# The MLP of a two-layer diffusion trunk in plain fp32: one product for three, hidden groups of 512 for 256

## The chip, the cores and the metric

The kernel runs on one core of one Trainium2 chip. The metric is the device time of one execution in microseconds. A core has a matrix engine (TensorE, PE in the rows, with PEld for its weight loads), a vector engine (DVE), a scalar engine (ACT), GpSimd (POOL) and SyncE (SP), which here issues nearly all the DMAs. Each engine runs its own program in order; they wait for one another through semaphores.

## What is computed

Two layers (DEPTH = 2) over 1152 tokens: 1024 latent ones and a prompt of 128, at D_MODEL = 1024 and a hidden width of 4096. A layer mixes the tokens (attention, mLSTM, neighbourhood attention, one output projection) and then runs the part that matters here:

```python
def squared_relu_mlp(h, w_up, w_down):
    return jnp.square(jax.nn.relu(h @ w_up)) @ w_down

def trunk_layer(x, mods, mixer, g_pre_mix, g_post_mix, g_pre_ffn, g_post_ffn, w_up, w_down):
    sh1, sc1, gt1, sh2, sc2, gt2 = mods
    mix_out, extras = mixer(rms_norm(x, g_pre_mix) * (1 + sc1) + sh1)
    x = x + gt1 * rms_norm(mix_out, g_post_mix)
    h = rms_norm(x, g_pre_ffn) * (1 + sc2) + sh2
    x = x + gt2 * rms_norm(squared_relu_mlp(h, w_up, w_down), g_post_ffn)
    return x, extras
```

All inputs, weights and outputs are fp32.

## The kernel before

The tokens lie in NT = 9 tiles of P = 128 (the prompt is the last), and D in KD = 8 slices of 128. The layers are one loop of two turns; within a layer, stages follow each other, each a block in which every engine has its own piece of program, with all engines meeting between blocks. The stages that the change touches come last in a layer:

- `out_projection` (L1612): turns the mixer's output, splits it into a high part (rounded to the type F32R) and a low part (what is left), and multiplies with W_out, split in the same way. At its end SP also loads the first 256 columns of W_up into `raw_up` (L1629); ACT and POOL split them (L1699, L1634), so that they lie ready for the MLP.
- `residual_norm("mix", 0, True)` (L457): a software pipeline over the nine tiles. For a tile, DVE scales the mixer's output (L557), adds the residual (L560), normalises (L567); PE turns the tile (L602); ACT and DVE modulate four of its eight slices each (L521, L575) into `full`, a buffer of three tiles. Then ACT copies the tile's high part into `hi` (L528) and DVE subtracts it to get `lo` (L582). Each step of a tile stands one turn of the loop behind the one ahead of it (ADD 1, SQUARES 2, NORM 3, MODULATE 4, HIGH 5, LOW 6).
- `mlp` (L1702): the hidden width goes in NG = 16 groups of HID = 256. In a group, six up tiles are made, each 128 hidden columns by 384 tokens, over KD = 8 slices; ACT takes relu (L1785) and square (L1787) and splits off the high part (L1789), DVE the low part (L1807). Then 18 down tiles, 128 tokens by 512 output columns, over KH = 2 slices, which DVE adds to `mix` (L1813). Each product of two fp32 operands is made by three F32R matmuls: high by high, high by low, low by high (L1755, L1769). The weights of a group have one buffer: SP loads them raw (L1723, L1726), ACT copies out the high parts (L1779, L1796) and POOL subtracts for the low parts (L1734, L1740); the next load waits for that. PE, ACT, DVE and POOL run the groups as loops; SP's issues are written out.
- `residual_norm("mlp", 1, False)`: the last residual add.

The three matmuls of an up product are:

```python
for k in range(KD):
    for a, b in ((up_hi, hi), (up_hi, lo), (up_lo, hi)):
        mm = pe.matmul(ps[:, j % 3, 0:384], a[:, k, m * P:(m + 1) * P], b[:, k, n * 384:(n + 1) * 384], ...)
```

Elsewhere the kernel multiplies plain fp32 operands by a single call, for example in the neighbourhood mixer's input projection (L1020, 128 columns of weights by 384 tokens over eight slices, six tiles a block, three blocks a layer), its v projection (L1027, 128 by 128) and the mLSTM's (L1167, as L1020).

Of the kernel before, what the change touches and what calls it, by code (L numbers as in the profile page):

```python
# [48 lines left out]
HID = 256  # L49
# [73 lines left out]
def build(nc, I, O):  # L123
    sems = {}
    with ExitStack() as ctx:
# [91 lines left out]
        with nc.Fori(0, DEPTH) as l:  # L217
# [239 lines left out]
            def residual_norm(tag, sub, norm):  # L457
# [4 lines left out]
                with ExitStack() as own:  # L462
# [4 lines left out]
                    FULL = 3  # L467
                    full = sb(f"{tag}_h_full", [P, FULL, KD, P], own) if norm else None
# [3 lines left out]
                    if norm:  # L472
                        x_sq, x_rstd = sem(f"{tag}_x_squares"), sem(f"{tag}_x_rstd")
                        normed, turned = sem(f"{tag}_normed"), sem(f"{tag}_turned")
                        mod_d, mod_a = sem(f"{tag}_modulated_dve"), sem(f"{tag}_modulated_act")
                        hi_done, lo_done = sem(f"{tag}_hi_done"), sem(f"{tag}_lo_done")
                    ON_DVE = 4

                    ADD, SQUARES, NORM, MODULATE, HIGH, LOW = 1, 2, 3, 4, 5, 6
                    STEPS = NT + (LOW if norm else ADD)  # L480
# [6 lines left out]
                    with nc.Block() as block:  # L487
# [17 lines left out]
                        def _(act):  # L505
# [9 lines left out]
                            def modulate(t):  # L515
                                c = 1 if t == PROMPT else 0
                                act.wait_ge(turned, t + 1)
                                if t >= FULL:
                                    act.wait_ge(lo_done, t - FULL + 1)
# [5 lines left out]
                            def high_part(t):  # L525
                                act.wait_ge(mod_a, t + 1)
                                act.wait_ge(mod_d, t + 1)
                                act.copy(hi[:, :, t * P:(t + 1) * P], full[:, t % FULL, :, :]).then_inc(hi_done, 1)  # L528

                            for n in range(STEPS):  # L530
                                if n < NT:
                                    squares_y(n)
                                if norm and 0 <= n - HIGH < NT:
                                    high_part(n - HIGH)
# [19 lines left out]
                        def _(dve):  # L554
# [14 lines left out]
                            def modulate(t):  # L569
                                c = 1 if t == PROMPT else 0  # L570
                                dve.wait_ge(turned, t + 1)
                                if t >= FULL:
                                    dve.wait_ge(lo_done, t - FULL + 1)
# [5 lines left out]
                            def low_part(t):  # L579
                                dve.wait_ge(hi_done, t + 1)  # L580
                                tt = slice(t * P, (t + 1) * P)
                                dve.tensor_tensor(lo[:, :, tt], full[:, t % FULL, :, :], hi[:, :, tt].bitcast(F32), ALU.subtract).then_inc(lo_done, 1)  # L582

                            for n in range(ADD, STEPS):
                                if n - ADD < NT:
                                    add_residual(n - ADD)
                                if norm and 0 <= n - LOW < NT:
                                    low_part(n - LOW)
# [1023 lines left out]
            def out_projection():  # L1612
# [5 lines left out]
                with ExitStack() as own:  # L1618
                    raw = sb("w_out_raw", [P, 2, KD, CUT], own)
                    w_hi = sb("w_out_hi", [P, 2, KD, CUT], own, F32R)  # L1620
                    w_lo = sb("w_out_lo", [P, 2, KD, CUT], own, F32R)
                    with nc.Block() as block:
                        @block.sync
                        def _(sp):
# [4 lines left out]
                            sp.dma_start(raw_up[:, :, :], w_up[:, :, 0:HID]).then_inc(sem("m_up_loaded"), 16)  # L1629

                        @block.gpsimd
                        def _(pool):
                            pool.wait_ge(sem("m_up_hi"), 1)
                            pool.tensor_tensor(up_lo[:, :, :], raw_up[:, :, :], up_hi[:, :, :].bitcast(F32), ALU.subtract).then_inc(sem("m_up_lo"), 1)  # L1634
# [41 lines left out]
                        def _(act):  # L1676
# [14 lines left out]
                            for j in range(NCUT * NT):  # L1691
# [5 lines left out]
                                if t == NT - 1 and c == NCUT - 2:  # L1697
                                    act.wait_ge(sem("m_up_loaded"), 16)
                                    act.copy(up_hi[:, :, :], raw_up[:, :, :]).then_inc(sem("m_up_hi"), 1)  # L1699


            def mlp():  # L1702
# [8 lines left out]
                with ExitStack() as own:  # L1711
                    raw_down = sb("w_down_raw", [P, KH, D], own)
                    down_hi, down_lo = (sb(f"w_down_{x}", [P, KH, D], own, F32R) for x in ("hi", "lo"))
                    u_hi, u_lo = (sb(f"u_{x}", [P, KH, TOK], own, F32R) for x in ("hi", "lo"))
                    relu = sb("relu", [P, 2, 384], own)
                    square = sb("square", [P, 2, 384], own)
                    with nc.Block() as block:
                        @block.sync
                        def _(sp):
                            for g in range(NG):  # L1720
                                if g >= 1:
                                    sp.wait_ge(sem("m_up_lo"), g)
                                    sp.dma_start(raw_up[:, :, :], w_up[:, :, g * HID:(g + 1) * HID]).then_inc(sem("m_up_loaded"), 16)  # L1723
                                if g >= 1:
                                    sp.wait_ge(sem("m_down_lo"), g)
                                sp.dma_start(raw_down[:, :, :], w_down[g]).then_inc(sem("m_down_loaded"), 16)  # L1726

                        @block.gpsimd
                        def _(pool):
                            pool.memset(mix[:, :, :], 0.0).then_inc(sem("m_out_cleared"), 1)  # L1730

                            def down_low(g):
                                pool.wait_ge(sem("m_down_hi"), g + 1)
                                pool.tensor_tensor(down_lo[:, :, :], raw_down[:, :, :], down_hi[:, :, :].bitcast(F32), ALU.subtract).then_inc(sem("m_down_lo"), 1)  # L1734

                            with pool.Fori(0, NG - 1) as g:
                                down_low(g)

# [162 lines left out]
```

## Time and profile before

| | before |
|---|---|
| time, median of 2 runs (lowest, highest) | 4337.26 us (4336.97, 4337.55) |
| span of the profiled execution | 4341.4 us |
| PE busy in it | 3953.9 us (91%) |
| DVE busy | 1637.1 us (38%) |
| ACT busy | 1242.6 us (29%) |
| POOL busy | 781.1 us (18%) |
| the costliest line, L1755 (up products), three groups | 515.0 + 514.6 + 514.4 us busy |
| L1769 (down products), three groups | 448.8 + 448.7 + 448.1 us busy |

The profiled execution's span is 4.1 us longer than the median. PE's busy times add up to more than the time that its matmuls fill, since successive matmuls overlap in the records: what a matmul costs in a stream is the interval from one start to the next, not its recorded duration. The rows give tenths of busy time in 40 slices, and the clock that the TensorE was granted (PEclk, as a share of 2.4 GHz; the other level is half of that).

### The profile page before, as it was taken

How to read it: one execution, taken by the hardware profiler on the slowest of the kernel's cores; microseconds unless marked ns; L12 is line 12 of the kernel's file. 1: busy time of each engine (PE TensorE's matmuls, PEld its weight loads, DVE VectorE, ACT ScalarE, POOL GpSimd, SP SyncE). 2: the span in 40 equal slices, each digit the busy share in tenths (PEclk: the TensorE clock that was granted, in tenths of full speed). 3: DMA queues.
4: the chain of work that ended last, by engine and by line, in shares of the span. 5: the costliest groups of instructions: out<-in, count | busy, mean ns of one | idle time of the engine just before them, and what ended most of it. 6: DMA issues, size and time to landing. Idle time of an engine off the chain costs nothing. (4 is left out here: it accounts for less than half of the span.)

```text
span 4341.4 us, 54476 instructions
## 1 busy us (share of the span) xinstructions
PE 3953.9 (91%) x21270; PEld 3248.0 (75%) x21270; DVE 1637.1 (38%) x3077; ACT 1242.6 (29%) x2544; POOL 781.1 (18%) x565
## 2 busy tenths in 40 slices
PE   6799999999697999999777999999896879999997
PEld 4477777674696999999644777777746869999996
DVE  1644333323716333333416443332237153333334
ACT  2233222212425222222222332222124242222222
POOL 0300111201304112121203001112013141211212
PEclk9899999999997999999887999899999979999998
DMA  6100111004113111111241001110041131111112
GB/s 204 52 1 1 44 44 28 25 19 156 31 41 111 42 39 48 39 39 48 84 158 52 1 1 44 44 32 29 13 155 31 50 105 39 39 48 39 48 39 87
DMA packets 189240, 233.44 MB, mean 54 GB/s; under 512 B 41522, under 2 KB 167092, under 8 KB 187444
## 3 DMA queue, kind: packets, MB, share of 16 engines
q1 hardware_dynamic: 188916, 231.04, 16.9%
q8 instruction: 112, 1.84, 0.2%
q14 instruction: 68, 0.56, 0.0%
q10 hardware_dynamic: 144, 0.01, 0.0%
HBM read 210.84 MB, written 32.71 MB: 56 GB/s over the span
## 5 line engine op out<-in xcount | busy, mean ns | idle before, releaser
L1813 DVE TENSOR_TENSOR mix<-mix,ps 128x512 f32<-128x512 f32 x576 | 395.3, 688 | 344.1 <-PE ps L1769 344.1
L1755 PE MATMUL ps<-h_hi,w_up_hi 128*128 128x384 f32 x1536 | 515.0, 335 | 10.0 <-PEq L487 10.0
L1755 PE MATMUL ps<-h_hi,w_up_lo 128*128 128x384 f32 x1536 | 514.6, 335 | 0.0
L1755 PE MATMUL ps<-h_lo,w_up_hi 128*128 128x384 f32 x1536 | 514.4, 335 | 0.0
L1769 PE MATMUL ps<-w_down_hi,u_lo 128*128 128x512 f32 x1152 | 448.8, 390 | 0.0
L1769 PE MATMUL ps<-w_down_lo,u_hi 128*128 128x512 f32 x1152 | 448.7, 390 | 0.0
L1769 PE MATMUL ps<-w_down_hi,u_hi 128*128 128x512 f32 x1152 | 448.1, 389 | 0.0
L1807 DVE TENSOR_TENSOR u_lo<-square,u_hi 128x384 fp32r<-128x384 f32 x192 | 133.5, 696 | 720.3 <-ACT u_hi L1789 720.3
L1755 PEld LDWEIGHTS ps<-h_hi,w_up_hi 128*128 128x128 f32 x1536 | 289.4, 188 | 11.9 <-issue 10.8
L1755 PEld LDWEIGHTS ps<-h_lo,w_up_hi 128*128 128x128 f32 x1536 | 289.4, 188 | 1.2
L1755 PEld LDWEIGHTS ps<-h_hi,w_up_lo 128*128 128x128 f32 x1536 | 289.1, 188 | 0.0
L1740 POOL TENSOR_TENSOR w_up_lo<-w_up_raw,w_up_hi 128x2048 fp32r<-128x2048 f32 x30 | 138.4, 4613 | 648.9 <-ACT w_up_hi L1796 648.9
L1769 PEld LDWEIGHTS ps<-w_down_hi,u_lo 128*128 128x128 f32 x1152 | 216.2, 188 | 45.0
L1769 PEld LDWEIGHTS ps<-w_down_lo,u_hi 128*128 128x128 f32 x1152 | 216.2, 188 | 44.4
L1769 PEld LDWEIGHTS ps<-w_down_hi,u_hi 128*128 128x128 f32 x1152 | 216.2, 188 | 44.2
L1734 POOL TENSOR_TENSOR w_down_lo<-w_down_raw,w_down_hi 128x2048 fp32r<-128x2048 f32 x32 | 147.6, 4611 | 552.5 <-ACT w_down_hi L1779 552.5
L1779 ACT CAST w_down_hi<-w_down_raw 128x2048 fp32r<-128x2048 f32 x32 | 61.2, 1914 | 647.0 <-PE ps L1769 633.5
L1785 ACT ACTIVATE relu<-ps 128x384 f32<-128x384 f32 x192 | 94.5, 492 | 476.5 <-PE ps L1755 476.5
L708 PE MATMUL ps<-a_v,attn_a_probsT 128*128 128x128 f32 x1752 | 217.7, 278 | 0.0
L708 PEld LDWEIGHTS ps<-a_v,attn_a_probsT 128*128 128x128 f32 x1752 | 209.5, 196 | 0.0
L753 DVE TENSOR_REDUCE small<-ps 128x1 f32<-128x1152 f32 (+1 forms) x120 | 137.4, 1145 | 188.4 <-PE ps L691 188.4
L1180 PE MATMUL ps<-ring,hT 128*128 128x256 f32 (+1 forms) x864 | 199.6, 391 | 1.5 <-PE ps L1180 1.2
(259 smaller groups left out, 6852.6 us busy)
## 6 DMA issues: line engine op xcount, KB each, us to landing
ring<-in_w_ada SPq DMA_DIRECT2D x32, 1024.0 KB, 5.3
w_up_raw<-in_w_ffn_up SPq DMA_DIRECT2D x32, 1024.0 KB, 5.5
w_down_raw<-in_w_ffn_down SPq DMA_DIRECT2D x32, 1024.0 KB, 4.9
w_ada_ring<-in_w_ada SPq DMA_DIRECT2D x16, 1024.0 KB, 9.6
c_window<-in_window SPq DMA_DIRECT2D x6, 1600.0 KB, 7.9
ring<-in_w_in SPq DMA_DIRECT2D x18, 512.0 KB, 5.2
in_x<-out_y_sample SPq DMA_DIRECT2D x16, 512.0 KB, 9.1
ring<-in_w_in SPq DMA_DIRECT2D x8, 1024.0 KB, 6.1
```

The lines of the kernel that those rows point to most:

```text
L708: mm = pe.matmul(out_p(i), PT[:, i % 2, k * P:(k + 1) * P], u["v"][k], start=(k == 0), stop=(k == u["n"] // P - 1))
L753: dve.tensor_reduce(nmax[:, i % 4:i % 4 + 1], S(i, 0, u["n"]), AX.X, ALU.max, negate=True).then_inc(max_ready, 1)
L1180: mm = pe.matmul(ps[:, j % 4, 0:n], hT[:, k, t * P:(t + 1) * P], ring[:, c % 2, k, 0:n], start=(k == 0), stop=(k == KD - 1))
L1734: pool.tensor_tensor(down_lo[:, :, :], raw_down[:, :, :], down_hi[:, :, :].bitcast(F32), ALU.subtract).then_inc(sem("m_down_lo"), 1)
L1740: pool.tensor_tensor(up_lo[:, :, :], raw_up[:, :, :], up_hi[:, :, :].bitcast(F32), ALU.subtract).then_inc(sem("m_up_lo"), 1)
L1755: mm = pe.matmul(ps[:, j % 3, 0:384], a[:, k, m * P:(m + 1) * P], b[:, k, n * 384:(n + 1) * 384], start=(k == 0 and a is up_hi and b is hi ...
L1769: mm = pe.matmul(ps[:, 3 + j % 5, :], a[:, k, t * P:(t + 1) * P], b[:, k, n * 512:(n + 1) * 512], start=(k == 0 and a is u_hi and b is dow ...
L1779: act.copy(down_hi[:, :, :], raw_down[:, :, :]).then_inc(sem("m_down_hi"), 1)
L1785: act.activation(relu[:, j % 2, :], ps[:, j % 3, 0:384], ACT.Relu).then_inc(sem("m_relu"), 1)
L1807: dve.tensor_tensor(u_lo[:, m, n * 384:(n + 1) * 384], square[:, j % 2, :], u_hi[:, m, n * 384:(n + 1) * 384].bitcast(F32), ALU.subtract). ...
L1813: dve.tensor_tensor(y, y, ps[:, 3 + j % 5, :], ALU.add).then_inc(sem("m_added"), 1)
```

## The change

The MLP's operands stay in plain fp32. `residual_norm` modulates straight into `h` and drops HIGH, LOW and the buffer `full`. `out_projection` keeps its own `hi` and `lo` and no longer loads or splits the MLP's first weights. `mlp` runs 8 groups of HID = 512, written out, with one matmul call per product, two buffers per weight (`w1`, `w2`), and neither splits nor low parts. Its first loads are issued at the start of its own block.

```diff
-HID = 256
+HID = 512
@@ residual_norm
-                    ADD, SQUARES, NORM, MODULATE, HIGH, LOW = 1, 2, 3, 4, 5, 6
-                    STEPS = NT + (LOW if norm else ADD)
+                    ADD, SQUARES, NORM, MODULATE = 1, 2, 3, 4
+                    STEPS = NT + (MODULATE if norm else ADD)
-                                    a = act.activation(full[:, t % FULL, k, :], turned_to(t, k), ACT.Identity,
+                                    a = act.activation(h[:, k, t * P:(t + 1) * P], turned_to(t, k), ACT.Identity,
-                                act.copy(hi[:, :, t * P:(t + 1) * P], full[:, t % FULL, :, :]).then_inc(hi_done, 1)
-                                    a = dve.tensor_scalar(full[:, t % FULL, k, :], turned_to(t, k), modT[:, 3, k, c:c + 1],
+                                    a = dve.tensor_scalar(h[:, k, t * P:(t + 1) * P], turned_to(t, k), modT[:, 3, k, c:c + 1],
-                                dve.tensor_tensor(lo[:, :, tt], full[:, t % FULL, :, :], hi[:, :, tt].bitcast(F32), ALU.subtract).then_inc(lo_done, 1)
@@ out_projection
-                            sp.dma_start(raw_up[:, :, :], w_up[:, :, 0:HID]).then_inc(sem("m_up_loaded"), 16)
-                            pool.tensor_tensor(up_lo[:, :, :], raw_up[:, :, :], up_hi[:, :, :].bitcast(F32), ALU.subtract).then_inc(sem("m_up_lo"), 1)
-                                    act.copy(up_hi[:, :, :], raw_up[:, :, :]).then_inc(sem("m_up_hi"), 1)
@@ mlp: loads
-                                    sp.wait_ge(sem("m_up_lo"), g)
-                                    sp.dma_start(raw_up[:, :, :], w_up[:, :, g * HID:(g + 1) * HID]).then_inc(sem("m_up_loaded"), 16)
-                                    sp.wait_ge(sem("m_down_lo"), g)
-                                sp.dma_start(raw_down[:, :, :], w_down[g]).then_inc(sem("m_down_loaded"), 16)
+                                if g >= 2:
+                                    sp.wait_ge(sem("m_up_done"), (g - 1) * UP)
+                                sp.dma_start(w1[:, g % 2, :, :], w_up[:, :, g * HID:(g + 1) * HID]).then_inc(sem(f"m_up_loaded{g % 2}"), 16)
+                                if g >= 2:
+                                    sp.wait_ge(sem("m_down_done"), (g - 1) * DOWN + 1)
+                                sp.dma_start(w2[:, g % 2, :, :], w_down[g]).then_inc(sem(f"m_down_loaded{g % 2}"), 16)
@@ mlp: tensor
-                            with pe.Fori(0, NG) as g:
-                                pe.wait_ge(sem("m_up_lo"), g + 1)
+                            for g in range(NG):
+                                pe.wait_ge(sem(f"m_up_loaded{g % 2}"), 16 * (g // 2 + 1))
-                                        for a, b in ((up_hi, hi), (up_hi, lo), (up_lo, hi)):
-                                            mm = pe.matmul(ps[:, j % 3, 0:384], a[:, k, m * P:(m + 1) * P], b[:, k, n * 384:(n + 1) * 384],
+                                        mm = pe.matmul(ps[:, j % 3, 0:384], w1[:, g % 2, k, m * P:(m + 1) * P], h[:, k, n * 384:(n + 1) * 384],
-                                        for a, b in ((u_hi, down_hi), (u_hi, down_lo), (u_lo, down_hi)):
-                                            mm = pe.matmul(ps[:, 3 + j % 5, :], a[:, k, t * P:(t + 1) * P], b[:, k, n * 512:(n + 1) * 512],
+                                        mm = pe.matmul(ps[:, 3 + j % 5, :], u[:, k, t * P:(t + 1) * P], w2[:, g % 2, k, n * 512:(n + 1) * 512],
@@ mlp: scalar and vector
-                                act.copy(down_hi[:, :, :], raw_down[:, :, :]).then_inc(sem("m_down_hi"), 1)
-                                    act.copy(u_hi[:, m, n * 384:(n + 1) * 384], square[:, j % 2, :]).then_inc(sem("m_u_hi"), 1)
+                                act.activation(u[:, m, n * 384:(n + 1) * 384], relu[:, j % 2, :], ACT.Square).then_inc(sem("m_squared"), 1)
-                                    dve.tensor_tensor(u_lo[:, m, n * 384:(n + 1) * 384], square[:, j % 2, :],
-                                                      u_hi[:, m, n * 384:(n + 1) * 384].bitcast(F32), ALU.subtract).then_inc(sem("m_u_lo"), 1)
```

PE's program from the turning of the last stage into the MLP, before (line numbers of each kernel; ISA is an instruction without a data tile):

```order
L602 MATMUL ps<-ident_sb,mix_x_normed 128x128 x72
L487 UNCONDITIONAL_BRANCH
L1743 UNCONDITIONAL_BRANCH
L1747 UNCONDITIONAL_BRANCH
L1747 ISA
L1755 MATMUL ps<-h_hi,w_up_hi 128x384
L1755 MATMUL ps<-h_lo,w_up_hi 128x384
L1755 MATMUL ps<-h_hi,w_up_lo 128x384
```

The same place in the changed kernel:

```order
L581 MATMUL ps<-ident_sb,mix_x_normed 128x128 x72
L484 UNCONDITIONAL_BRANCH
L1703 UNCONDITIONAL_BRANCH
L1714 MATMUL ps<-h,w_up 128x384 x96
L1727 MATMUL ps<-w_down,u 128x512 x72
```

The loop over groups is gone, and a group is 96 up calls (12 tiles of 8) and 72 down calls (18 tiles of 4), where a group of half the width was 144 and 108.

SP's program where the MLP's block begins, before:

```order
L494 DMA out_y_prompt<-mix_x 128x1024
L487 UNCONDITIONAL_BRANCH
L1718 UNCONDITIONAL_BRANCH
L1726 ISA
L1726 DMA w_down_raw<-in_w_ffn_down 128x2x1024
L1723 ISA
L1723 DMA w_up_raw<-in_w_ffn_up 128x8x256
```

And in the changed kernel:

```order
L491 DMA out_y_prompt<-mix_x 128x1024
L484 UNCONDITIONAL_BRANCH
L1689 UNCONDITIONAL_BRANCH
L1694 ISA
L1694 DMA w_up<-in_w_ffn_up 128x8x512
L1697 DMA w_down<-in_w_ffn_down 128x4x1024
```

The first up weights of a layer, which stood at the end of `out_projection`, are now the first DMA of the MLP's block, and twice as large; three more DMAs of 2 MB follow without a wait between them.

DVE's program in `residual_norm("mix")`, one turn of the pipeline, before:

```order
L557 SCALAR_TENSOR_TENSOR mix<-mix,small,gate 128x1024
L560 TENSOR_TENSOR mix_x<-mix_x,mix 128x1024
L582 TENSOR_TENSOR h_lo<-mix_h_full,h_hi 128x8x128
L567 TENSOR_SCALAR mix_x_normed<-mix_x,small 128x1024
L575 TENSOR_SCALAR mix_h_full<-ps,modT 128x128 x4
```

And its end in the changed kernel, from the last tile's turn on:

```order
L545 SCALAR_TENSOR_TENSOR mix<-mix,small,gate 128x1024
L548 TENSOR_TENSOR mix_x<-mix_x,mix 128x1024
L555 TENSOR_SCALAR mix_x_normed<-mix_x,small 128x1024
L561 TENSOR_SCALAR h<-ps,modT 128x128 x4
L555 TENSOR_SCALAR mix_x_normed<-mix_x,small 128x1024
L561 TENSOR_SCALAR h<-ps,modT 128x128 x4
L555 TENSOR_SCALAR mix_x_normed<-mix_x,small 128x1024
L561 TENSOR_SCALAR h<-ps,modT 128x128 x8
```

The nine subtractions (L582) are gone, and the pipeline is two turns shorter.

## Rows read from the trace of the kernel before

**Rows 1.** The page: span, PE, the 40 slices of PE and its clock.

```profile
span 4341.4 us, 54476 instructions
PE   6799999999697999999777999999896879999997
PEclk9899999999997999999887999899999979999998
```

**Rows 2.** Stretches: residual_norm("mix"), MLP, last add, for both layers (busy us, records).

```profile
core 0: us, PE busy (x) PEld busy (x) DVE busy (x) ACT busy (x) POOL busy (x), PEclk, DMA share, GB/s
1295.00:1349.60 54.60, 17.72 (x72) 14.12 (x72) 49.81 (x72) 42.43 (x81) 30.89 (x37) 0.53 0.49 173
1349.60:2143.50 793.90, 793.81 (x4032) 725.44 (x4032) 262.39 (x384) 205.03 (x319) 150.38 (x32) 1.00 0.13 41
...
3516.90:4310.80 793.90, 793.87 (x4032) 725.50 (x4032) 262.44 (x383) 205.03 (x319) 150.35 (x32) 1.00 0.13 41
```

**Rows 3.** Waits: engine, line, waited for: us in total, times, longest us.

```profile
ACT relu L1785 <- PE ps L1755: 476.5, 190, 2.6
DVE mix L1813 <- PE ps L1769: 344.1, 512, 0.7
```

**Rows 4.** One group's up and down lines, the next group's start: ns min/median/max, starts.

```profile
L1755 PE MATMUL ps<-h_hi,w_up_hi x48: 333/334/346, 1549.2 to 1573.7; 128*128 128x384 f32 x48
...
L1769 PE MATMUL ps<-w_down_hi,u_hi x36: 387/389/390, 1574.2 to 1598.0; 128*128 128x512 f32 x36
...
L1755 PE MATMUL ps<-h_hi,w_up_hi x3: 333/334/346, 1598.7 to 1599.8; 128*128 128x384 f32 x3
```

**Rows 5.** Plain fp32 lines: all of L1020, then one block each of L1020 and L1027.

```profile
L1020 PE MATMUL ps<-hT,ring x576: 486/486/562, 463.2 to 2909.0; 128*128 128x384 f32 x192
...
L1020 PE MATMUL ps<-hT,ring x96: 486/486/562, 463.2 to 493.9; 128*128 128x384 f32 x96
...
L1027 PE MATMUL ps<-ring,hT x144: 273/275/275, 494.2 to 510.2; 128*128 128x128 f32 x144
```

**Rows 6.** The stretch of one block of L1020 (columns as in rows 2).

```profile
464.00:493.00 29.00, 29.00 (x92) 17.07 (x91) 5.55 (x10) 6.71 (x14) 0.00 (x0) 1.00 0.46 103
```

**Rows 7.** Timeline where the first MLP begins: start, us, engine, line, [idle before].

```profile
1349.37 0.41 SPq L1726 DMA_DIRECT2D w_down_raw<-in_w_ffn_down  x1
...
1349.64 0.68 PE L1755 MATMUL ps<-h_hi,w_up_hi 128*128 128x384 f32 x1 [4.98 <-PEq L487]
...
1349.96 0.41 SPq L1723 DMA_DIRECT2D w_up_raw<-in_w_ffn_up  x1
1350.12 0.52 PE L1755 MATMUL ps<-h_lo,w_up_hi 128*128 128x384 f32 x1
```

**Rows 8.** Those two DMA issues: KB each, us from issue to landing.

```profile
w_down_raw<-in_w_ffn_down SPq DMA_DIRECT2D x1, 1024.0 KB, 5.0
...
w_up_raw<-in_w_ffn_up SPq DMA_DIRECT2D x1, 1024.0 KB, 7.6
```

**Rows 9.** DVE in residual_norm("mix"), first layer: turns of five tiles, one subtraction, the last.

```profile
1306.25 1.29 DVE L557 SCALAR_TENSOR_TENSOR mix<-mix,small,gate 128x1024 f32<-128x1024 f32 x1 [0.44 <-POOL small L545]
...
1311.18 1.28 DVE L557 SCALAR_TENSOR_TENSOR mix<-mix,small,gate 128x1024 f32<-128x1024 f32 x1
...
1315.58 1.28 DVE L557 SCALAR_TENSOR_TENSOR mix<-mix,small,gate 128x1024 f32<-128x1024 f32 x1
...
1326.63 1.27 DVE L557 SCALAR_TENSOR_TENSOR mix<-mix,small,gate 128x1024 f32<-128x1024 f32 x1
...
1329.08 1.22 DVE L582 TENSOR_TENSOR h_lo<-mix_h_full,h_hi 128x1024 fp32r<-128x1024 f32 x1
1330.22 0.75 DVE L567 TENSOR_SCALAR mix_x_normed<-mix_x,small 128x1024 f32<-128x1024 f32 x1
...
1332.16 1.28 DVE L557 SCALAR_TENSOR_TENSOR mix<-mix,small,gate 128x1024 f32<-128x1024 f32 x1
...
1347.72 1.23 DVE L582 TENSOR_TENSOR h_lo<-mix_h_full,h_hi 128x1024 fp32r<-128x1024 f32 x1 [0.26 <-ACT h_hi L528]
```

More of the change, by code:

```diff
@@ L466, in residual_norm @@
                     xn = sb(f"{tag}_x_normed", [P, 2, D], own) if norm else None
-                    FULL = 3
-                    full = sb(f"{tag}_h_full", [P, FULL, KD, P], own) if norm else None
                     ssq, rstd = small[:, 0:NT], small[:, NT:2 * NT]
@@ L1621, in out_projection @@
                     w_lo = sb("w_out_lo", [P, 2, KD, CUT], own, F32R)
+                    hi = sb("o_mixT_hi", [P, KD, TOK], own, F32R)
+                    lo = sb("o_mixT_lo", [P, KD, TOK], own, F32R)
                     with nc.Block() as block:
@@ L1711, in mlp @@
                 with ExitStack() as own:
-                    raw_down = sb("w_down_raw", [P, KH, D], own)
-                    down_hi, down_lo = (sb(f"w_down_{x}", [P, KH, D], own, F32R) for x in ("hi", "lo"))
-                    u_hi, u_lo = (sb(f"u_{x}", [P, KH, TOK], own, F32R) for x in ("hi", "lo"))
+                    w2 = sb("w_down", [P, 2, KH, D], own)
+                    u = sb("u", [P, KH, TOK], own)
                     relu = sb("relu", [P, 2, 384], own)
-                    square = sb("square", [P, 2, 384], own)
                     with nc.Block() as block:
@@ L1774, in _ @@
                         def _(act):
[L1775 to L1797 removed]
+                            for j in range(NG * UP):
+                                i = j % UP
+                                n, m = i // KH, i % KH
+                                act.wait_ge(sem("m_up_done"), j + 1)
+                                act.activation(relu[:, j % 2, :], ps[:, i % 3, 0:384], ACT.Relu).then_inc(sem("m_relu"), 1)
+                                act.wait_ge(sem("m_relu"), j + 1)
+                                act.activation(u[:, m, n * 384:(n + 1) * 384], relu[:, j % 2, :], ACT.Square).then_inc(sem("m_squared"), 1)
                         @block.vector
@@ L1802, in _ @@
                             dve.sem_inc(sem("m_added"), 1)
-                            with dve.Fori(0, NG) as g:
-                                for j in range(UP):
-                                    n, m = j // KH, j % KH
-                                    dve.wait_ge(sem("m_u_hi"), g * UP + j + 1)
-                                    dve.tensor_tensor(u_lo[:, m, n * 384:(n + 1) * 384], square[:, j % 2, :],
-                                                      u_hi[:, m, n * 384:(n + 1) * 384].bitcast(F32), ALU.subtract).then_inc(sem("m_u_lo"), 1)
+                            for g in range(NG):
                                 for j in range(DOWN):
@@ L1830, in build @@
             mlp_memory = ExitStack()
-            hi = sb("h_hi", [P, KD, TOK], mlp_memory, F32R)
-            lo = sb("h_lo", [P, KD, TOK], mlp_memory, F32R)
-            raw_up = sb("w_up_raw", [P, KD, HID], mlp_memory)
-            up_hi, up_lo = (sb(f"w_up_{x}", [P, KD, HID], mlp_memory, F32R) for x in ("hi", "lo"))
             w_up = I["w_ffn_up"][l].rearrange("(k p) n -> p k n", p=P)
```

58 lines of the change are left out of this document (6 added, 52 removed).

## The prediction

> **What bounds the kernel now.** I read the page first: PE is busy for nearly the whole span, and the slices show two long plateaus at 9 with a full clock [rows 1]. Then the stretches by stage: each layer has an MLP of 793.9 us in which PE is busy for 793.8 us at a granted clock of 1.00 (the 2.4 GHz level), while DVE is busy for 262 us, ACT for 205 and POOL for 150 [rows 2]. Two MLPs are 1588 us of the 4341. The waits say the same from the other side: ACT waited for an up tile 190 times (there are 2 x 16 x 6 = 192 of them), DVE for a down tile 512 times of 576 [rows 3]. So in the MLP nothing but the length of PE's stream counts, and every split that ACT, DVE and POOL lose there is worth nothing by itself: PE hides it today.
>
> The stage ahead of it, `residual_norm("mix")`, is 54.6 us a layer with DVE busy for 49.8 and PE for 17.7 [rows 2]. There DVE's length counts.
>
> **What a product costs in PE's stream.** Durations overlap, so I take intervals between starts. Before: a group's up part runs from 1549.2 to the first down matmul at 1574.2, 25.0 us for 48 products, 0.521 us each (three F32R matmuls of 384 columns); its down part from there to the next group at 1598.7, 24.5 us for 36 products, 0.681 us each (three of 512 columns) [rows 4]. A layer has 768 up products and 576 down products, before and after: 768 x 0.521 + 576 x 0.681 = 400.1 + 392.3 = 792.4 us, which is the 793.9 of the stretch but for a slow start of 1.5.
>
> After: one plain fp32 call for each. The kernel has such calls elsewhere, L1020 with the very shape of an up product. In the program that line is called 8 x 6 times a block in six blocks, 288 times; the trace has 576 records [rows 5]. A plain call is thus two records. In one block the 96 records run from 463.2 to 493.9, so 30.7 / 95 = 0.323 us from one to the next, at a granted clock of 1.00 and with PE busy throughout [rows 5, 6]. An up product therefore costs 2 x 0.323 = 0.646 us, against 0.521: 24% more, not a third of it.
>
> For a down product no dense plain row of 512 columns exists, so I bound it. In L1027, 128 columns wide, 144 records take 494.2 to 510.2, 0.112 us each [rows 5]. The line through 128 and 384 columns gives 0.323 + (0.323 - 0.112) / 2 = 0.429 at 512; scaling the 384-column row by 512/384 gives 0.431. A far upper end is two F32R records of that width, 2 x 0.227 = 0.454; but at 384 columns two of them cost 0.347 and the plain record only 0.323. I take 0.430, from the plain rows: 0.860 us a product, against 0.681.
>
> One page speaks against the change before any row is read. The Trainium skill, in "FP8 and Floating Point Precision", section "TensorE Precision Notes", says that a true fp32 product takes four passes through the array (each high and low part by each). By that page an estimate at 2.4 GHz is 4 x 384 / 2.4 = 0.640 us for an up product and 0.853 for a down one, 983 us a layer. The trace agrees within 1% for the shape that it has: 0.646 measured on L1020.
>
> **The sum for PE's stream.** After: 768 x 0.646 + 576 x 0.860 = 496.1 + 495.4 = 991.5 us. The difference to 792.4 is 199.1 us a layer, 398 us for both. Bounds: 0.322 to 0.324 (starts are given to 0.1 us) and 0.429 to 0.431 make the stream 989 to 994 us, +196 to +202 a layer; with the far end of 0.454 it is 1019, +227.
>
> What must stay hidden behind it: ACT has one relu and one square for an up tile that now lasts 8 x 0.646 = 5.2 us, less work than in the 205 us of before; DVE has 144 adds a layer in place of 288 and no subtractions, against 262 us busy of before [rows 2]. Loads: a group now lasts 124 us, and its 4 MB went in two such groups of before with the DMAs 13% busy [rows 2]; with two buffers they are issued a group ahead. The removed splits, the loop of PE that is written out and the DVE adds cost or give nothing here.
>
> **The start of the MLP.** Today PE starts 0.27 us after SP's first issue in the block (1349.64 against 1349.37), since the up weights already lie there [rows 7]. After, PE waits for 2 MB issued at that point. The two 1 MB loads there landed 5.0 us after their issues at 1349.37 and 7.6 after 1349.96, that is at 1354.4 and 1357.6: the second MB took 3.2 us more [rows 7, 8]. So 2 MB land about 8.2 us after the issue, and PE starts 8 us later than now. The first load was not held up by the one issued 0.6 us behind it, so I count nothing for the three loads behind. Were all 8 MB to share the way evenly, the first would land at 5.0 + 7 x 3.2 = 27.4 us: +27. Range +7 to +27, taken +8: 16 us for both layers. PE's first two records there are 0.48 us apart, against 25.0 / 144 = 0.174 later [rows 4, 7], and the stage ahead ran at a mean granted clock of 0.53, near the 1.2 GHz level [rows 2]: a longer pause finds the clock already low, so nothing is added for it. Nothing else is issued behind PE's wait but the MLP itself.
>
> The loads and splits taken out of `out_projection` lie beside PE's stream there, so they give nothing.
>
> **The stage before it.** DVE loses nine subtractions. One takes 1.14 us of its queue (1329.08 to 1330.22). With one in it, a turn takes 5.53 us (1326.63 to 1332.16); the two turns just ahead of the first one took 4.93 and 4.40 (from 1306.25 over 1311.18 to 1315.58) [rows 9]. So the three later turns of the pipeline shrink by 0.6 to 1.13 us each, 1.8 to 3.4, and behind the last scaling (1332.16) six subtractions fall away, 6.8 us, of which the chain of the last tile (square, root, normalise, turn, modulate) can keep some: I count 6.0. Together 9.4 us a layer; at least 5, at most 9 x 1.14 + 0.7 of waiting = 11. For both layers -19.
>
> **Sum.** 4341.4 + 398 + 16 - 19 = 4736 us of span. The profiled execution is 4.1 us above the median, so 4732 us, 9.1% slower.
>
> **Rivals.**
> - *As forecast*: 4732, own range 4720 to 4756 (stream +196 to +202, start +7 to +12, stage -11 to -5, each twice, hardly all at one end). All rows of a dense plain stream agree with it. Chance 0.82.
> - *The first weights share the DMA engines with the three loads behind*: +27 in place of +8 a layer, 4732 + 38 = 4770. For it: four 2 MB loads are issued at once, and rows 8 has only two. Against it: there the first was not delayed. Chance 0.06.
> - *A down record costs as much as two F32R ones*, 0.454 us: +28 a layer, 4732 + 56 = 4788. Against it: the 384-column rows. Chance 0.03.
> - *PE pauses between parts of the written-out stream* (a wait on squares, on adds, or on its own instructions): with 1.4 us at each of 16 seams of a layer it is +45, 4777. Against it: in L1020 and L1027, written out too, records follow each other without gaps. Chance 0.06.
> - *Faster: a plain call costs half*, one record in place of two, because the MLP's operands are fed as L1755's are. Then the stream is 768 x 0.323 + 576 x 0.430 = 496 us, 4341 - 593 - 3 - 4 = 3741. It decides from 0.80 of the rows' price on (792.4 / 991.5): below that the change gains. For it: one call stands where three stood, and the weight loads fall to a third. Against it: 576 records for 288 calls of just this type and shape. Chance 0.02; between this and the forecast, near no change, 0.01.
>
> **How the numbers follow.** The time is that of the likeliest case. The range, 4710 to 4780, takes in the forecast's own and the two likelier of the slower rivals, and some 10 us below for the stage before the MLP, whose gain is the least certain term. About 2% (87 us) is what a measurement of this kernel can tell from no change: faster 0.02, same 0.01, slower 0.97.
>
> **What would show it.** In the profile after, the MLP's stretch should be about 993 us with PE busy throughout, 1536 up records a layer at 0.323 us and 1152 down records at 0.430; PE's first MLP matmul some 8 us after SP's first issue; the stage ahead of it about 45 us from its first load to its last modulation. ACT's waits for up tiles should grow. Wrong would be the forecast if the records of a call are not two, if their intervals differ from L1020's, if the first load takes over 12 us, or if PE stands idle between groups.

## The result, and the profile after

The changed kernel takes 4728.97 us against 4337.26 us: 1.0897 times as long, with a 95% interval of 1.0877 to 1.0918. The forecast was 4732 us with a range of 4710 to 4780.

The page of the changed kernel: its span, the 40 slices of PE and of PE's clock, and the two lines of the MLP (busy us, mean ns of one, idle before):

```profile
span 4727.3 us, 45986 instructions
...
PE   7799999987979999999877999999978799999997
...
PEclk9799999989979999999987998999989899999998
...
L1714 PE MATMUL ps<-h,w_up 128*128 128x384 f32 x3072 | 998.7, 488 | 20.2 <-DMA w_up<-in_w_ffn_up 20.2
...
L1727 PE MATMUL ps<-w_down,u 128*128 128x512 f32 x2304 | 991.4, 592 | 0.0
```

The program calls line 1714 2 x 768 times and line 1727 2 x 576 times. The page has 3072 and 2304 records, two for each call, as L1020 had [rows 5]. The plateaus at 9 are the two MLPs; they are longer than before [rows 1], and the clock in them is as high.

The stretches of the first layer: stage before the MLP, wait for the weights, MLP, start of the last add (columns as in rows 2):

```profile
core 0: us, PE busy (x) PEld busy (x) DVE busy (x) ACT busy (x) POOL busy (x), PEclk, DMA share, GB/s
1295.70:1339.80 44.10, 16.81 (x72) 13.41 (x72) 39.59 (x63) 33.67 (x72) 29.48 (x37) 0.57 0.59 215
1339.80:1347.90 8.10, 0.00 (x1) 0.01 (x1) 0.00 (x0) 0.00 (x0) 7.72 (x1) 0.50 0.86 304
1347.90:2339.60 991.70, 991.70 (x2686) 511.82 (x2687) 98.30 (x143) 97.33 (x192) 0.00 (x0) 1.00 0.09 32
```

In this stretch of the MLP PE is busy for 991.70 of 991.70 us at a granted clock of 1.00, while DVE and ACT are at about 98 us each. Before, the like stretch was 793.90 us with DVE at 262 and ACT at 205 [rows 2]. The other engines lost over half of their work there, and yet the MLP became 199 us longer: from PE's first matmul to the next stage's first issue it takes 993.8 us (1347.90 to 2341.69), where it took 794.8 (1349.64 to 2144.46).

PE's timeline over one group and the next (start, us, line, count):

```profile
1598.21 62.08 PE L1714 MATMUL ps<-h,w_up 128*128 128x384 f32 x192
1660.13 61.96 PE L1727 MATMUL ps<-w_down,u 128*128 128x512 f32 x144
1721.93 62.08 PE L1714 MATMUL ps<-h,w_up 128*128 128x384 f32 x192
```

From start to start an up part takes 61.92 us for 192 records, 0.3225 us each; a down part 61.80 us for 144, 0.429 us each. No idle time stands between the parts.

The waits (engine, line, waited for: us in total, times, longest us):

```profile
DVE mix L1750 <- PE ps L1727: 1806.1, 288, 77.1
ACT relu L1737 <- PE ps L1714: 1679.9, 192, 65.9
```

Against 344.1 and 476.5 us before [rows 3]: with their splits gone and PE's stream longer, DVE and ACT mostly wait for PE.

Where the first MLP begins (start, us, engine, line, [idle before <-releaser]):

```profile
1339.88 0.41 SPq L1694 DMA_DIRECT2D w_up<-in_w_ffn_up  x1
1340.38 0.53 SPq L1697 DMA_DIRECT2D w_down<-in_w_ffn_down  x1
1341.10 0.37 SPq L1694 DMA_DIRECT2D w_up<-in_w_ffn_up  x1
1341.66 7.96 SPq L1697 DMA_DIRECT2D w_down<-in_w_ffn_down  x1
1347.90 1.65 PE L1714 MATMUL ps<-h,w_up 128*128 128x384 f32 x2 [10.08 <-DMA w_up<-in_w_ffn_up]
```

PE starts 8.02 us after the first issue; before it was 0.27 [rows 7]. The landing of that first load (issued at 1339.88, three more behind it), and of the up load issued by itself at 1413.02 (KB, us from issue to landing):

```profile
w_up<-in_w_ffn_up SPq DMA_DIRECT2D x1, 2048.0 KB, 8.0
...
w_up<-in_w_ffn_up SPq DMA_DIRECT2D x1, 2048.0 KB, 8.0
```

The three loads behind the first one did not delay it.

For the whole account, SP's first issue of each stage, first of the kernel before (its first MLP's, 1349.37, stands in rows 7), then of the changed one (its first MLP's, 1339.88, stands above):

```profile
1295.05 0.35 SPq L491 DMA_DIRECT2D mix_x<-out_y_sample  x1
2144.46 0.83 SPq L491 DMA_DIRECT2D mlp_x<-out_y_sample  x2
3462.39 0.83 SPq L491 DMA_DIRECT2D mix_x<-out_y_sample  x2
3516.66 0.41 SPq L1726 DMA_DIRECT2D w_down_raw<-in_w_ffn_down  x1
4311.80 0.35 SPq L491 DMA_DIRECT2D mlp_x<-out_y_sample  x1
```

```profile
1295.71 0.35 SPq L488 DMA_DIRECT2D mix_x<-out_y_sample  x1
2341.69 0.35 SPq L488 DMA_DIRECT2D mlp_x<-out_y_sample  x1
3651.87 0.35 SPq L488 DMA_DIRECT2D mix_x<-out_y_sample  x1
3695.82 0.41 SPq L1694 DMA_DIRECT2D w_up<-in_w_ffn_up  x1
4697.32 0.35 SPq L488 DMA_DIRECT2D mlp_x<-out_y_sample  x1
```

Their differences divide the span without a rest:

| part of the span, us | before | after | difference | forecast |
|---|---|---|---|---|
| up to the first residual_norm("mix") | 1295.05 | 1295.71 | +0.7 | 0 |
| residual_norm("mix"), two layers | 54.32 + 54.27 | 44.17 + 43.95 | -20.5 | -19 |
| MLP from its first issue to the next stage's, two layers | 795.09 + 795.14 | 1001.81 + 1001.50 | +413.1 | +398 + 16 |
| from there to the second layer's residual_norm("mix") | 1317.93 | 1310.18 | -7.8 | 0 |
| behind the last MLP | 29.60 | 29.98 | +0.4 | 0 |
| span | 4341.4 | 4727.3 | +385.9 | +395 |

### The profile page after: what moved, and what is told of

The parts are those of the page before. It is cut to its first block and busy times, and to the rows that moved or that the text cites. A ratio compares the mean times of both kernels' runs of the same rounds, so it can differ in the third digit from the quotient of the medians.

```text
span 4727.3 us, 45986 instructions
## 1 busy us (share of the span) xinstructions
PE 4346.0 (92%) x18582; PEld 2817.4 (60%) x18582; DVE 1287.6 (27%) x2579; ACT 1005.3 (21%) x2270; POOL 483.1 (10%) x501
## 5 line engine op out<-in xcount | busy, mean ns | idle before, releaser
L1714 PE MATMUL ps<-h,w_up 128*128 128x384 f32 x3072 | 998.7, 488 | 20.2 <-DMA w_up<-in_w_ffn_up 20.2
L1727 PE MATMUL ps<-w_down,u 128*128 128x512 f32 x2304 | 991.4, 592 | 0.0
L1714 PEld LDWEIGHTS ps<-h,w_up 128*128 128x128 f32 x3072 | 586.1, 191 | 432.7 <-DMA w_up<-in_w_ffn_up 20.6
L1727 PEld LDWEIGHTS ps<-w_down,u 128*128 128x128 f32 x2304 | 437.8, 190 | 547.6 <-issue 543.4
L1750 DVE TENSOR_TENSOR mix<-mix,ps 128x512 f32<-128x512 f32 x288 | 197.9, 687 | 1806.1 <-PE ps L1727 1806.1
L999 PE MATMUL ps<-hT,ring 128*128 128x384 f32 x576 | 187.2, 487 | 7.9 <-PEq L147 7.9
L1159 PEld LDWEIGHTS ps<-ring,hT 128*128 128x128 f32 x864 | 166.0, 194 | 30.7 <-issue 4.2
L1631 PE MATMUL ps<-w_out_hi,o_mixT_hi 128*128 128x256 f32 x576 | 163.2, 283 | 0.0
L1631 PE MATMUL ps<-w_out_lo,o_mixT_hi 128*128 128x256 f32 x576 | 163.0, 283 | 0.0
L1631 PE MATMUL ps<-w_out_hi,o_mixT_lo 128*128 128x256 f32 x576 | 163.0, 283 | 0.0
```

The lines of the kernel that those rows point to most:

```text
L999: mm = pe.matmul(ps[:, j % 3, 0:384], ring[:, slot, k, m * P:(m + 1) * P], hT[:, k, n * 384:(n + 1) * 384], start=(k == 0), stop=(k == KD ...
L1159: mm = pe.matmul(ps[:, j % 4, 0:n], hT[:, k, t * P:(t + 1) * P], ring[:, c % 2, k, 0:n], start=(k == 0), stop=(k == KD - 1))
L1631: mm = pe.matmul(ps[:, 4 + j % 4, 0:CUT], a[:, k, tt], b[:, c % 2, k, :], start=(k == 0 and a is hi and b is w_hi), stop=(k == KD - 1 and ...
L1714: mm = pe.matmul(ps[:, j % 3, 0:384], w1[:, g % 2, k, m * P:(m + 1) * P], h[:, k, n * 384:(n + 1) * 384], start=(k == 0), stop=(k == KD - 1))
L1727: mm = pe.matmul(ps[:, 3 + j % 5, :], u[:, k, t * P:(t + 1) * P], w2[:, g % 2, k, n * 512:(n + 1) * 512], start=(k == 0), stop=(k == KH - 1))
L1750: dve.tensor_tensor(y, y, ps[:, 3 + j % 5, :], ALU.add).then_inc(sem("m_added"), 1)
```

## The experiments

The theory was that PE's stream of records sets the MLP's time, that a plain fp32 call is two records of about twice an F32R record's length, and that the rest of the change (group size, buffers, loads, splits) moves only the edges. The rivals: the larger groups and their loads cost the time; PE's interval is stretched by the splits beside it; the start is dear for another reason than the load.

**The group size alone.** The changed kernel with the groups of before:

```diff
-HID = 512
+HID = 256
```

> The changed kernel with hidden groups of 256 as before the change: only the type of the products and the two buffers stay. If the loss is the price of a plain product in TensorE's stream, the MLP keeps about 991 us a layer of matmuls (768 x 0.646 + 576 x 0.860), and only the first load shrinks from 2 MB to 1 MB, landing 3 us earlier a layer: 4729 - 6 = 4723 us. If the larger groups or their loads bear the loss, the time goes back by a good part of the 392 us, under 4600.

Measured: 4724.11 us, 1.0887 times the kernel before (1.0868 to 1.0905). It is 4.9 us less than with groups of 512, which fits the sooner start: the smaller first load lets PE begin 5.54 us after the issue (1345.26 against 1339.72) in place of 8.02, twice. The four runs lie 11 us apart, so the 4.9 by itself shows little. So the group size does not explain the 392 us. The two buffers stay in this run; the next one keeps them too, and the loss goes all the same.

**The form of the call alone.** Groups of 256 and two buffers stay, but each product is again three F32R calls. ACT rounds the weights; the low parts are left out, and the three calls repeat the product of the rounded operands:

```diff
-w2 = sb("w_down", [P, 2, KH, D], own)
+w2 = sb("w_down", [P, 2, KH, D], own, F32R)
...
-mm = pe.matmul(ps[:, j % 3, 0:384], w1[...], h[...], start=(k == 0), stop=(k == KD - 1))
+for i in range(3):
+    mm = pe.matmul(ps[:, j % 3, 0:384], w1[...], h[...],
+                   start=(k == 0 and i == 0), stop=(k == KD - 1 and i == 2))
```

> The changed kernel in groups of 256, with three F32R calls on the same rounded operands in place of one plain call (weights rounded by ACT as they come in; the low parts are left out, so that two of the three products are repeats of the first). Everything else of the change stands. If the type of the record is the cause, the MLP falls to 768 x 0.521 + 576 x 0.681 = 792 us a layer and the first start is load 5 + rounding 2 us: 4729 - 2 x 199 - 2 = 4329 us. If the cause lies in groups, buffers or the written-out stream, it stays near 4720.

Measured: 4346.24 us, 1.0017 times the kernel before (1.0006 to 1.0028), 17 us over what was expected, but 378 us under the same kernel with plain calls. PE's timeline in it:

```profile
1377.21 24.68 PE L1730 MATMUL ps<-w_down,u 128*128 128x512 f32 x108
1401.74 23.59 PE L1716 MATMUL ps<-h,w_up 128*128 128x384 f32 x135
```

A down part takes 24.53 us for 108 records, 0.227 us each, as in the kernel before [rows 4], although nothing is split here. The price follows the form of the call, and neither groups nor buffers bear it. The 17 us come from elsewhere for the most part. A layer's MLP takes 802.9 us from its first issue (1342.61) to the next stage's (2145.49), 1.2 us more than the sum had it (1001.7 - 199 - 1), the load and the rounding ahead of PE's start included. Beside the changed kernel's, the second layer's mixer, which no edit touches, took 8.0 us longer (1318.15 against 1310.18), the two stages ahead of the MLP 4.3 us together (46.3 and 46.1 against 44.2 and 44.0), and what stands behind the last MLP 3.5 us (33.5 against 30.0). Why these differ was not tried.

**The start alone.** The first up weights are loaded one stage earlier, behind the first six x tiles:

```diff
 for t in range(SLOTS):
     sp.dma_start(x[:, t % SLOTS, :], x_tile(t)).then_inc(sem(f"{tag}_x_loaded{t}"), 16)
+if norm:
+    sp.dma_start(w1[:, 0, :, :], w_up[:, :, 0:HID]).then_inc(sem("m_up_loaded0"), 16)
...
-residual_norm("mix", 0, True)
 w1 = sb("w_up", [P, 2, KD, HID], mlp_memory)
+residual_norm("mix", 0, True)
```

> The changed kernel with the first up weights of a layer loaded in the stage ahead of the MLP, behind its first six loads of x. If PE's wait at the start of the MLP is those 8 us and nothing else, it goes: 4729 - 2 x 7.9 = 4713 us. If the 2 MB take the way of the loads of x that the stage needs, the stage grows by up to the 6 us that 2 MB take, and 4717 to 4725 is left.

Measured: 4712.74 us, ratio 1.0863 (1.0845 to 1.0881), 16.2 us less than the changed kernel. The start of the first MLP in it:

```profile
1340.11 0.41 SPq L1700 DMA_DIRECT2D w_down<-in_w_ffn_down  x1
1340.16 10.31 PE L1717 MATMUL ps<-h,w_up 128*128 128x384 f32 x26 [2.12 <-PEq L484]
```

PE starts 0.05 us after SP's first issue, not 8.02 after it. By their issues the two MLPs became 9.1 and 8.8 us shorter (992.73 each), 8 of them the wait. The other 1 us is a slow start: the first up part takes 63.7 us in this run (1340.16 to 1403.84) and 64.8 in the changed kernel (1347.90 to 1412.69), against 61.92 later on. The second layer's mixer was 1.4 us longer this time, so the times differ by little more than twice 8. The wait was the load, and the early load cost the x tiles nothing that shows: the stage ahead took 44.1 us in both layers.

**One F32R call for each product.** As the kernel of three calls, with the loop of three taken away, here in the down product and likewise in the up product; the low parts are left out:

```diff
-for i in range(3):
-    mm = pe.matmul(ps[:, 3 + j % 5, :], u[...], w2[...],
-                   start=(k == 0 and i == 0), stop=(k == KH - 1 and i == 2))
+mm = pe.matmul(ps[:, 3 + j % 5, :], u[...], w2[...], start=(k == 0), stop=(k == KH - 1))
```

> As the run with three F32R calls, but one call per product (operands rounded to F32R, low parts left out). If records of F32R cost 0.1736 us at 384 columns and 0.2269 at 512 whatever stands beside them, the MLP is 768 x 0.1736 + 576 x 0.2269 = 264 us a layer, 4729 - 2 x 728 - 2 = 3271 us. If another engine takes over (DVE has 12.4 us of adds in a group of 16.5, ACT about 10, each 1 MB load 5 us and its rounding 2), it stands above 3300.

Measured: 3313.88 us, ratio 0.7639 (0.7626 to 0.7652), 43 us over what was expected. Two stretches of one group, up and down part (columns as in rows 2):

```profile
1366.84:1375.16 8.32, 8.32 (x49) 8.32 (x48) 2.36 (x4) 6.27 (x10) 0.00 (x0) 1.00 0.13 32
1375.16:1384.31 9.15, 9.15 (x37) 6.22 (x37) 8.48 (x15) 3.01 (x5) 0.00 (x0) 1.00 0.55 202
```

The line of the down part's additions (ns min/median/max, first and last start):

```profile
L1769 DVE TENSOR_TENSOR mix<-mix,ps x576: 676/677/689, 1358.4 to 3279.3; 128x512 f32<-128x512 f32 x192
```

The up part is on its records: 8.32 / 48 = 0.1733 us. The down part is not: 9.15 / 36 = 0.254 in place of 0.227. A tile of it is now two records, 0.454 us, and DVE's addition of a tile takes 0.677, so DVE is behind, and the weight loads wait for it (engine, line, waited for: us in total, times, longest us):

```profile
PEld ps L1728 <- DVE mix L1769: 53.1, 192, 0.3
```

The excess is 16 x (9.15 - 36 x 0.227) = 16 us a layer, 31 of the 43 us; the other 12 were not broken down. The cover that the forecast of the changed kernel counted on (DVE's additions behind PE's stream) ends where a tile's records are shorter than 0.68 us. A group of 512 columns has four records a tile, so this reading can be put to the test, which the last experiment does.

**The splits alone.** The kernel before, its subtractions (DVE and POOL) cut to one column, in the same way for the down weights and the squared tiles; the three products read the high parts:

```diff
-dve.tensor_tensor(lo[:, :, tt], full[:, t % FULL, :, :], hi[:, :, tt].bitcast(F32), ALU.subtract)
+dve.tensor_tensor(lo[:, 0, t * P:t * P + 1], full[:, t % FULL, 0, 0:1], hi[:, 0, t * P:t * P + 1].bitcast(F32), ALU.subtract)
...
-pool.tensor_tensor(up_lo[:, :, :], raw_up[:, :, :], up_hi[:, :, :].bitcast(F32), ALU.subtract)
+pool.tensor_tensor(up_lo[:, 0, 0:1], raw_up[:, 0, 0:1], up_hi[:, 0, 0:1].bitcast(F32), ALU.subtract)
```

> The kernel before, with the subtractions that make the low parts cut to one column (on VectorE in the stage of the residual and norm and behind each squared tile, on GpSimd for the weights); the three products then all read the high parts, so the low parts are left out of the result. Theory (the splits are hidden behind TensorE in the MLP, and cost only VectorE turns in the stage before it): the MLP stays at its 792 us of records, the stage loses what it lost in the changed kernel (10.15 us a layer), so 4337 - 20 = 4317 us, 4310 to 4325. Rival A (VectorE's and GpSimd's reading and writing beside the matmuls stretches the records from 384 / 2.4 = 160 ns to 173.6 and from 213 to 226.9): the MLP falls to 2304 x 0.160 + 1728 x 0.213 = 737 us a layer and the time to about 4205 us. Rival B (the stage's 10 us do not come from the splits but from the moved load or the target's shape): 4337 us.

Measured: 4334.06 us, ratio 0.9979 (0.9960 to 0.9998): some 9 us gained by the ratio, 6 by the medians (4340.5 us for the kernel before beside it), not 20. Its stretches, stage and MLP:

```profile
1294.20:1343.20 49.00, 17.70 (x72) 14.12 (x72) 40.56 (x72) 42.39 (x81) 27.23 (x37) 0.52 0.52 193
1343.70:2137.60 793.90, 793.90 (x4032) 725.75 (x4032) 211.73 (x383) 204.87 (x319) 13.11 (x32) 1.00 0.13 41
```

In the MLP POOL went from 150 to 13 us and DVE from 262 to 212, and PE has as many records in a stretch of the same length as before [rows 2]. From PE's first matmul to the next stage's first issue the MLP took 795.1 us (1343.70 to 2138.83) against 794.8. The splits were hidden there, and they do not stretch the records: rival A falls. In the stage ahead only half of the 10 us came. The end of that stage, ACT and DVE's last record:

```profile
1337.60 1.50 ACT L521 ACTIVATE mix_h_full<-ps,modT 128x128 f32<-128x128 f32 x4
1339.13 1.04 ACT L528 CAST h_hi<-mix_h_full 128x1024 fp32r<-128x1024 f32 x1
1340.08 1.50 ACT L521 ACTIVATE mix_h_full<-ps,modT 128x128 f32<-128x128 f32 x4
1341.61 1.04 ACT L528 CAST h_hi<-mix_h_full 128x1024 fp32r<-128x1024 f32 x1
...
1342.69 0.16 DVE L582 TENSOR_TENSOR h_lo<-mix_h_full,h_hi 128x1 fp32r<-128x1 f32 x1 [2.32 <-ACT h_hi L528]
```

With DVE relieved, the last tiles go at ACT's pace: a scaling and a high copy, 2.48 us a tile, and DVE waits 2.32 us for it. The changed kernel has no high copy either, and there ACT's last eight scalings stand in one row:

```profile
1336.58 2.90 ACT L516 ACTIVATE h<-ps,modT 128x128 f32<-128x128 f32 x8 [0.44 <-PE ps L581]
```

So the subtractions alone are worth 5 us a layer. That the other 5 belong to ACT's copies (and the steps of the pipeline that wait for them) is argued from these rows; no run takes out the copies alone.

**Three F32R calls at 128 columns.** As the kernel of three calls, with up tiles of 128 tokens in place of 384:

```diff
-UP = 3 * KH
+UP = NT * KH
...
-mm = pe.matmul(ps[:, j % 3, 0:384], w1[...], h[:, k, n * 384:(n + 1) * 384], ...)
+mm = pe.matmul(ps[:, j % 3, 0:P], w1[...], h[:, k, n * P:(n + 1) * P], ...)
```

> As e_f32r3 (three F32R calls on the rounded operands, low parts left out), but with up tiles of 128 tokens in place of 384: 2304 up products a layer, each of 3 records. Theory (an F32R record costs its columns at 2.4 GHz and 13 ns more): 128 / 2.4 + 13.3 = 66.7 ns, 6912 x 0.0667 = 461 us a layer against 400 us at 384 columns, so 4346 + 2 x 61 = 4468 us; the plain call of 128 columns that the kernel before shows (2 x 0.112 = 0.224 us) would then still lie over three F32R calls (0.200 us). Rival (at 128 columns the weight load of each record sets the pace, as in the plain records of 0.112 us): 6912 x 0.112 = 774 us a layer, 4346 + 2 x 374 = 5094 us, and the plain call would be the cheaper one by a third at this width.

Measured: 5173.65 us, ratio 1.1910 (1.1840 to 1.1979). The theory of a fixed 13 ns on top of the columns falls. Stretches of the first layer: first up part in two halves, first down part, second up part:

```profile
1350.60:1395.00 44.40, 44.40 (x208) 44.40 (x209) 0.00 (x0) 10.16 (x19) 0.00 (x0) 0.50 0.29 95
1395.00:1442.80 47.80, 47.80 (x226) 47.80 (x226) 0.00 (x0) 5.27 (x18) 0.00 (x0) 0.50 0.00 1
1442.80:1468.90 26.10, 26.10 (x109) 21.45 (x110) 11.69 (x17) 0.59 (x2) 0.00 (x0) 0.94 0.00 1
1468.90:1517.10 48.20, 48.20 (x434) 48.19 (x432) 0.69 (x1) 13.56 (x36) 0.00 (x0) 1.00 0.14 45
```

In the second group an up part takes 48.20 us for 432 records, 0.112 us each, as much as a plain record of 128 columns [rows 5]. At this width three F32R calls cost 0.335 us and a plain call 0.224; the rival's price was right. For F32R it is more than the columns ask for: the line through its records of 384 and 512 columns (0.1735 and 0.227) would give 0.067 at 128. The plain records show no such excess: the line through 0.3225 and 0.429 gives 0.109. That the weight load sets the pace of the F32R records is therefore likely, but it is argued and not shown: the weight loads (PEld) are busy for all of this stretch, yet they are so too in F32R's up parts of 384 columns (8.32 of 8.32 us above), which go at 0.1733 a record. The price of the plain call needs no such reason. A layer has 16 x 48.2 = 771 us of up parts against 400, +742 us for two; the other 85 us are nearly all the first group's: it ran at a granted clock of 0.50 (the 1.2 GHz level) for 92 us, 44 us more than the second, in both layers.

The Trainium skill states a price for a weight load: "TensorE: Matmul & The Clock Gate", section "LDWEIGHTS (loading the stationary operand)", gives columns / 1.2 in ns, by which 128 columns cost 107 ns. The 112 ns of the trace agree within 5 at a granted clock of 1.00; in the first group, at 0.50, a record took 213 ns (92.2 us / 432), which that price does not give.

**One F32R call in groups of 512, with the early load.** The low parts are left out as before; the down weights are rounded in two halves, and the roundings stand behind a group's last up tile:

```diff
-HID = 256
+HID = 512
...
+if norm:
+    sp.dma_start(raw1[:, :, :], w_up[:, :, 0:HID]).then_inc(sem("m_up_loaded"), 16)
...
+if i == UP - 1 and j // UP + 1 < NG:
+    round_up(j // UP + 1)
+    round_down(j // UP + 1, 0)
+    round_down(j // UP + 1, 1)
```

> As e_f32r1 (one F32R call for each product on operands rounded to F32R, low parts left out), but in groups of 512 columns, with the first up weights loaded behind the first x tiles of the stage before, and the roundings of the weights behind a group's last up tile. Theory (in e_f32r1 the down part runs at VectorE's pace, one addition of 0.677 us against 2 records of 0.227): with 4 records a tile (0.908 us) TensorE sets the pace again, 576 x 0.227 = 130.7 us a layer in place of 16 x 9.15 = 146.4, and the first product comes 5 us earlier: 3313.9 - 2 x (15.7 + 5) = 3272 us. Rival (another cost holds the down part back, the PSUM reads or the loads): the down part stays, and only the early load shows: about 3304 us.

Measured: 3274.3 us, ratio 0.7543 (0.7504 to 0.7582), 2 us from what was expected. The stretches of an up and a down part:

```profile
1377.78:1394.44 16.66, 16.66 (x97) 16.66 (x96) 0.69 (x1) 11.21 (x22) 0.00 (x0) 1.00 0.16 63
1394.44:1410.80 16.36, 16.36 (x73) 13.52 (x73) 11.70 (x17) 8.26 (x5) 0.00 (x0) 1.00 0.53 193
```

The down part is back at 16.36 / 72 = 0.227 us a record: with four records a tile, 0.91 us, DVE's 0.68 is hidden again. The loads are not what held the part back before: the DMAs are about as busy in it now (0.53) as then (0.55). The roundings were moved in the same run, so what they did is not told apart from what the four records did. The first product comes 3.5 us after SP's first issue (1342.38 against 1338.85) in place of 7.4. It is the fastest of the kernels here, but with operands that are rounded to F32R, where the kernel before keeps the low parts and the changed one the whole fp32 operands. It is no replacement where that accuracy is wanted.

## Why the prediction was right, step by step

**What bounds the kernel.** Right. In the changed kernel PE is busy for all of the MLP, and taking the subtractions out of the kernel before moved its MLP by less than 1 us a layer.

**The price of a product.** Right, and this step carries the result. The forecast took 0.323 us for an up record from L1020 and 0.430 for a down record by extending the plain rows; measured were 0.3225 and 0.429. That makes 768 x 0.645 + 576 x 0.858 = 990 us a layer against the forecast's 991.5, and the stretch is 991.70. The far end, 0.454 (two F32R records), did not occur, nor did the faster rival: the records are two for a call. The Trainium skill's four passes ("FP8 and Floating Point Precision", section "TensorE Precision Notes") gave an estimate of 983 us a layer; the trace agrees within 1%, with two records a call, each near 2 x 384 / 2.4 = 320 ns at 384 columns.

**The start.** Right: 8.02 us against 8. The loads behind the first one did not delay it, so the rival of shared engines (+27) fell, and the early load took 16.2 us off the time again. One term was put at nothing and is not: "a longer pause finds the clock already low, so nothing is added for it". The granted clock was 0.50 when PE began, in the changed kernel as in the run with the early load. But the first up part lost 2.9 and 2.5 us against a later one in the changed kernel, and 1.8 us in each layer with the early load: behind the longer pause the start was about 1 us a layer slower.

**The stage before.** Right in size (10.2 and 10.3 us a layer against 9.4), wrong in its ground. The forecast booked all of it on DVE's nine subtractions, among them "six subtractions fall away, 6.8 us" behind the last scaling, and named ACT nowhere in that step. With the subtractions alone away only 5.2 and 5.4 us came, as ACT's scaling and high copy take 2.48 us a tile there. The size held, it seems, since the change removes those copies as well, which the forecast did not count on: here the number was partly luck. The last row of rows 9 had the hint: DVE's last subtraction waited 0.26 us for `h_hi`, so at the end of the stage ACT was already the one waited for.

**Seams of the written-out loop.** Counted at nothing, and nothing is there: PE's starts follow each other over the parts without idle time.

**From span to time.** The step held, though its 4.1 us were misread. By the table the changed parts came to 413.1 - 20.5 = 392.6 us against 395 forecast, and the medians of the two kernels lie 391.7 apart. The spans differ by 385.9 only, since the second layer's unchanged mixer was 7.8 us shorter. The profiled execution of before was a long one: each run with span and time on record has a time 1.6 to 1.7 us over its span, which puts that execution at an estimated 4343 us, 5.8 over the median. The forecast set its span against the median of times and read 4.1. But taking off whatever the one execution had over the median makes the forecast the median plus 395, which is 4732, and so the long mixer is not in it. What is left, 3 us, is 2.4 of the changed parts and 1 of the rest. That the rest is so small is luck, with runs of the kernel before 18 us and more apart; the table's rows for the MLP are not.

## What to carry to other kernels

Price a change of operand type by the interval between records of the same type and width in the trace, and count the records for a call: at 384 and 512 columns a plain fp32 call (0.645 and 0.858 us) cost 24 to 26% more than three F32R calls, while at 128 columns, where a record of either kind took 0.112 us, it would be a third cheaper. Splitting work on engines that waited for TensorE anyway cost nothing here, so taking it away gained nothing; what it did cost stood in the stage where those engines are the bound, and there relieving the busiest alone gave half. When TensorE's part is cut, look at once for the next duration per tile: here it was an addition of 0.68 us, and larger groups hid it again.

## What the runs showed that was not expected

**An unchanged block is not the same length each time.** Two neighbouring blocks of the second layer's mixer in the kernel before (columns as in rows 2):

```profile
2623.50:2746.50 123.00, 117.94 (x637) 89.36 (x638) 42.67 (x126) 35.10 (x77) 25.07 (x17) 0.93 0.17 39
2746.50:2878.40 131.90, 126.91 (x637) 96.57 (x638) 42.93 (x126) 34.80 (x77) 25.00 (x17) 0.86 0.16 36
```

Two such blocks in the changed kernel:

```profile
2818.84:2944.78 125.94, 120.90 (x637) 91.76 (x638) 42.73 (x126) 34.94 (x77) 25.05 (x17) 0.91 0.16 38
2944.78:3067.90 123.12, 117.91 (x637) 89.39 (x638) 42.62 (x126) 35.04 (x77) 25.05 (x17) 0.93 0.16 39
```

The same 637 PE records took 123.0 us at a mean granted clock of 0.93 and 131.9 at 0.86; in the changed kernel they took 123.1 to 125.9. Over the nine profiled kernels the second layer's mixer, which no change touches, took 1310.2 to 1311.5 us in five, 1315.4 in one and 1317.9 to 1318.5 in three. The three long ones are the three kernels with three F32R calls a product at 384 and 512 columns, but with one profile of each that may be chance. What decides it stays open; no experiment here was aimed at it. It is as large as several terms of the forecast, so a term of a few us is checked in its own stretch, not in the total.

**TensorE can stay at half clock while it is busy.** At 128 columns of F32R the first up part of each layer ran at a granted clock of 0.50 for 92 us with PE and PEld busy throughout, and rose only in the part of 512 columns behind it; the same up part in the second group ran at 1.00. With 384 columns the first up part of the kernel of three calls had this mean:

```profile
1350.50:1377.20 26.70, 26.70 (x144) 26.70 (x145) 0.00 (x0) 10.59 (x13) 0.00 (x0) 0.93 0.47 158
```

At 384 columns the clock was up again soon after the start. Why 128 columns keep it high in the second group and do not raise it in the first was not tried.
